# One decoder block kernel on one core: the front runs into the inversion without a barrier, two kinds of small transfers change queue, and value rows change places with a norm

## The reference

```python
p = rmsnorm(x, norm_mix) @ w_in            # 1024 -> 2048 (retention) + 1824 (RWKV)
q = rope(q, positions); k = rope(k, positions) * HEAD_DIM ** -0.5   # retention
# RWKV-7, one step per token
sa = einsum('bhvk,bhk->bhv', state, a_t)
state = state * w_t + sa[..., None] * b_t + v_t[..., None] * k_t
# second block: differential attention normalizes q and k over 32 features
q = rmsnorm_2(q, g_q); k = rmsnorm_2(k, g_k)
s = q @ k.T * scale + _t5_bias(table, dist)
```

## Time and profile before

| | us |
|---|---|
| median of three timed runs | 1727.69 (1725.25 to 1728.7) |
| the profiled execution, its own time | 1724.9 |
| its span in the trace | 1723.0 |
| busy in the span: PE, DVE, ACT, POOL | 1633.6, 902.3, 660.9, 75.7 |
| shares of the chain that ended last: PE, DVE, ACT, DMA | 82%, 6%, 6%, 1% |

### The profile page before, as it was taken

The page is one execution under the profiler, slowest core; times in us unless marked ns, Lnnn a source line. Parts: engine busy times, 40 slices in busy tenths (PEclk is TensorE's granted clock), DMA queues, the critical chain, the costliest instruction groups (busy, mean ns, idle before and its releaser), DMA issues.

```text
span 1723.0 us, 25989 instructions
## 1 busy us (share of the span) xinstructions
PE 1633.6 (95%) x11207; PEld 1311.3 (76%) x11207; DVE 902.3 (52%) x1404; ACT 660.9 (38%) x990; POOL 75.7 (4%) x105
## 2 busy tenths in 40 slices
PE   7899988999998999999999999996889999999998
PEld 5766768977796778888888777775557788888887
DVE  6444567515444355555454645434864765555544
ACT  3215931234434254333241435444775422222220
POOL 1300100000000000000000200002300000000000
PEclk9999998999999999999999999996989999999999
DMA  6612141003242344536363341420002233333322
GB/s 210 172 49 73 52 150 33 4 5 112 82 147 74 107 143 149 193 119 208 113 220 122 122 130 56 99 73 25 1 13 72 65 102 95 96 103 93 98 86 86
DMA packets 150692, 170.28 MB, mean 99 GB/s; under 512 B 14297, under 2 KB 111203, under 8 KB 150195
## 3 DMA queue, kind: packets, MB, share of 16 engines
q1 hardware_dynamic: 141080, 151.58, 27.7%
q10 hardware_dynamic: 9498, 17.06, 3.5%
HBM read 164.12 MB, written 6.33 MB: 99 GB/s over the span
## 4 chain that ended last, share of the span: by engine, by line
PE 82%; DVE 6%; ACT 6%; issue 2%; ACTq 1%; DMA 1%; POOL 1%; DVEq 0%; POOLq 0%; SPq 0%
PE ps L389 64%; PE ps L1250 4%; PE ps L1410 2%; PE ps L2371 1%; DVE weights_low L412 1%; PE ps L2383 1%; PE ps L2559 1%; ACT weights_high L409 1%; PE ps L2394 1%; PE ps L1636 1%; ACT sb_hT L2474 1%; DMA sb_arena<-sb_arena 1%; PE ps L894 1%; PE ps L906 1%; ACT sb_arena L671 1%
## 5 line engine op out<-in xcount | busy, mean ns | idle before, releaser
L389 PE MATMUL ps<-left_high,weights_high 128*128 128x512 f32 (+1 forms) x1016 | 403.4, 397 | 7.9 <-DVE left_low L693 3.3
L412 DVE TENSOR_TENSOR weights_low<-sb_weights_raw,weights_high 128x2048 fp32r<-128x2048 f32 (+1 forms) x118 | 265.2, 2248 | 260.7 <-ACT weights_high L409 260.6
L389 PE MATMUL ps<-left_high,weights_low 128*128 128x512 f32 (+1 forms) x1016 | 395.8, 390 | 0.0
L389 PE MATMUL ps<-left_low,weights_high 128*128 128x512 f32 (+1 forms) x1016 | 395.7, 389 | 0.0
L409 ACT CAST weights_high<-sb_weights_raw 128x2048 fp32r<-128x2048 f32 (+1 forms) x118 | 221.4, 1876 | 348.9 <-PE ps L389 294.0
L389 PEld LDWEIGHTS ps<-left_high,weights_high 128*128 128x128 f32 (+1 forms) x1016 | 190.0, 187 | 63.4 <-issue 13.4
L389 PEld LDWEIGHTS ps<-left_high,weights_low 128*128 128x128 f32 (+1 forms) x1016 | 190.1, 187 | 41.0
L389 PEld LDWEIGHTS ps<-left_low,weights_high 128*128 128x128 f32 (+1 forms) x1016 | 190.2, 187 | 40.3 <-issue 1.7
L389 PE MATMUL ps<-weights_high,hidden_high 128*128 128x512 f32 x432 | 169.0, 391 | 0.0
L389 PE MATMUL ps<-weights_high,hidden_low 128*128 128x512 f32 x432 | 168.2, 389 | 0.0
L389 PE MATMUL ps<-weights_low,hidden_high 128*128 128x512 f32 x432 | 168.1, 389 | 0.0
(11 more groups left out here) (394 smaller groups left out, 2134.3 us busy)
## 6 DMA issues: line engine op xcount, KB each, us to landing
sb_weights_raw<-in_w_in SPq DMA_DIRECT2D x25, 1024.0 KB, 5.3
sb_yT<-in_ada_w SPq DMA_DIRECT2D x24, 1024.0 KB, 5.2
sb_weights_raw<-in_ffn_w_up SPq DMA_DIRECT2D x44, 512.0 KB, 4.7
sb_weights_raw<-in_mlp_w_up SPq DMA_DIRECT2D x16, 1024.0 KB, 6.3
sb_weights_raw<-in_mlp_w_down SPq DMA_DIRECT2D x16, 1024.0 KB, 7.6
sb_weights_raw<-in_ffn_w_down SPq DMA_DIRECT2D x10, 1024.0 KB, 5.0
sb_weights_raw<-in_xattn_w_kv SPq DMA_DIRECT2D x8, 1024.0 KB, 5.1
sb_weights_raw<-in_w_out SPq DMA_DIRECT2D x6, 1024.0 KB, 5.0
```

What stands on the lines that cost most here:

```text
L389: last = nc.tensor.matmul(o, lhsT, rhs, start=b["first"] and i == 0, stop=b["last"] and i == len(pairs) - 1)
L412: nc.vector.tensor_tensor(l[:, 0:n], raw[:, 0:n], h[:, 0:n].bitcast(F32), ALU.subtract).then_inc(w_low, 1)
```

## The change

The edits are five.

- The barrier between the front and the inversion is gone on the three engines. In its place stand waits: TensorE waits for ScalarE's copies of the last two chunks, and before each u for a count `removal_ready`, which VectorE raises once per BT tile and once per bonus tile (u 0 and 1 need one and two, u 2 and 3 all eight). The bonus sums lie in banks 2, 3, 6 and 7 instead of 2 to 5, since u 0 and 1 write banks 0, 4, 1 and 5. ScalarE waits for the last product of `w_in` before the two gate DMAs.
- The eight DMAs of the skewed table are issued by SyncE, ahead of the third chunk of `w_q`.
- The four DMAs of the keys' exchange are issued by SyncE, behind the load of chunk 7 of `w_in`. Those of the queries stay with ScalarE.
- ScalarE takes its 18 steps there in one piece.
- VectorE takes five dense steps behind each of the two norms, where it took two.

```diff
         def bonus_pe(pe, f):
...
-            nc.tensor.matmul(ps[:, 2 + f, :], sum64, BON_IN[:, f % 2, :], start=True, stop=True).then_inc(bonus_sum, 1)
+            nc.tensor.matmul(ps[:, BONUS_BANK[f], :], sum64, BON_IN[:, f % 2, :], start=True,
+                             stop=True).then_inc(bonus_sum, 1)
...
-            swap_act(a, 0)
-            fill(dense, 8)
-            swap_act(a, 1)
-            fill(dense, 10)
+            exchange_halves(a, a.eng, 0)
+            fill(dense, 18)
...
         def invert_pe(pe):
+            for n in (-2, -1):
+                kept_by_act(pe, w_in, n)
             for u in range(NPAIR):
+
+                pe.wait_ge(removal_ready, (u + 1, u + 1, 8, 8)[u])
                 chunk_products(u, of_cols(BT), of_cols(AT), u).then_inc(inv_gram, 1)
...
         def invert_act(a):
+            a.wait_ge(acc_done, w_in[-1]["blocks"][-1]["acc"])
             a.eng.dma_start(GUP0, A["rwkv_g_up"][0, 0:P]).then_inc(front_loaded, 16)
             a.eng.dma_start(GUP1[0:32], A["rwkv_g_up"][0, P:P + 32]).then_inc(front_loaded, 16)
-            skew_bias_act(a)
...
-                fill(dense, 2)
+                fill(dense, 5)
...
-            stream_weights(sp, STREAM[1:])
+            stream_weights(sp, STREAM[1:8])
+            exchange_halves(sp, sp, 1)
+            stream_weights(sp, STREAM[8:w_qkv[2]["index"]])
+            skew_bias_sp(sp)
+            stream_weights(sp, STREAM[w_qkv[2]["index"]:])
...
             front1_pe(pe)
-            pe.stage_end()
             invert_pe(pe)
```

More of the change, by code:

```diff
@@ L542, in store_bias_act, with skew_bias_sp @@
             a.eng.dma_start(bias_dram, VECS[0:8]).then_inc(bias_stored, 16)
-        def skew_bias_act(a):
+        def skew_bias_sp(sp):
+            sp.wait_ge(bias_stored, 16)
             for h in range(8):
@@ L548, in skew_bias_act @@
                 rows = bass.AP(tensor=bias_dram.tensor, offset=h * VEC, ap=[[0, P], [1, VEC]])
-                a.eng.dma_start(skewed, rows).then_inc(bias_stored, 16)
+                sp.dma_start(skewed, rows).then_inc(bias_stored, 16)
         def load_params_sp(sp):
@@ L839, in rot_tile @@
             return (QT, KTt)[n // 4][:, n % 4, :]
-        def swap_act(a, q_or_k):
+        def exchange_halves(side, queue, q_or_k):
             src = (QT, KTt)[q_or_k]
-            kept_by_act(a, w_in, 2 * q_or_k + 1)
+            kept_by_act(side, w_in, 2 * q_or_k + 1)
             if q_or_k:
-                a.wait_ge(rotated, 4)
+                side.wait_ge(rotated, 4)
             for to in range(0, P, 32):
                 frm = to + 32 if to % 64 == 0 else to - 32
-                a.eng.dma_start(EXCHANGED[to:to + 32], src[frm:frm + 32]).then_inc(swapped, 16)
+                queue.dma_start(EXCHANGED[to:to + 32], src[frm:frm + 32]).then_inc(swapped, 16)
         def rotate_dve(v, n):
@@ L977, in build_program @@
         (lora_in, lora_w, lora_a, sig_w, sig_a, kk_squared, kk_scaled, kk_sum, kk_floor,
[L978 removed]
+         removal_ready, kk_rstd, key_scale, key_scaled, cum_ready, before_ready, decay_w, decay_before, decay_inv, bonus_in,
          bonus_sum) = (sem("rwkv_" + n) for n in (
              "lora_in", "lora_w", "lora_a", "sig_w", "sig_a", "kk_squared",
[L981 removed]
+             "kk_scaled", "kk_sum", "kk_floor", "removal_ready", "kk_rstd", "key_scale", "key_scaled", "cum_ready", "before_ready",
              "decay_w", "decay_before", "decay_inverse", "bonus_in", "bonus_sum"))
@@ L1080, in removal_dve @@
             v.wait_ge(decay_inv, f + 1)
-            nc.vector.tensor_tensor(BT[:, f, :], AA[:, f, :], WI[:, f, :], ALU.mult)
+            nc.vector.tensor_tensor(BT[:, f, :], AA[:, f, :], WI[:, f, :], ALU.mult).then_inc(removal_ready, 1)
         def receptance_dve(v, f):
@@ L1095, in receptance_dve @@
             nc.vector.tensor_tensor(KTW[:, f, :], KTW[:, f, :], WI[:, f, :], ALU.mult)
+        BONUS_BANK = (2, 3, 6, 7)
         def bonus_pe(pe, f):
@@ L1105, in bonus_dve @@
             v.wait_ge(acc_done, w_in[-1]["blocks"][-1]["acc"])
-            nc.vector.tensor_tensor(BON[:, f, :], ps[:, 2 + f, :], VT[:, f, :], ALU.mult)
+            nc.vector.tensor_tensor(BON[:, f, :], ps[:, BONUS_BANK[f], :], VT[:, f, :], ALU.mult).then_inc(removal_ready, 1)
         def front1_pe(pe):
@@ L3061, in _ @@
             front1_act(a)
-            a.stage_end()
             invert_act(a)
```

3 lines of the change are left out of this document (removed).

## The result

| | before | changed |
|---|---|---|
| median, us | 1727.49 | 1715.34 |
| lowest to highest, us | 1725.25 to 1728.70 | 1711.92 to 1717.84 |
| profiled execution, us | 1724.9 | 1717.84 |
| its span, us | 1723.0 | 1716.0 |

The account below looks back on a forecast made before the run. The prediction took TensorE, with 82% of the chain, to bound the kernel, with gains only where it waits. Its terms -9.0 - 6.9 + 1.4 = -14.5 us gave 1713.2 us against the 1727.69 median, 8-in-10 range 1707 to 1719.5.

Parts of the forecast that it names:

- the forecast's own case: Whole kernel: the predicted 1713.2 us, own range 1709 to 1717.5, chance 0.65.
- Two of the signs that the forecast named for being wrong: Retention starting before 90 or after 95; attention stage longer by more than 2 us; a third was a `w_q` wait.
- The norm, -9.0: Second norm: copies placed before it shorten TensorE's idle time from 11.7 to 3.1 us; 9.0 us less.
- The inversion, -6.9: Inversion's start: VectorE starts at 246.5 instead of 253.40, 6.2 us from the table DMAs, the rest from the barrier.
- the forecast's upper bound: Inversion's start: at most 7.8 us gained, if the gate DMAs too were off the path.
- The tables on SyncE, 0: SyncE's queue near `w_q`: eight table copies delay no weights; third chunk lands about 437, cast at 451.22; cost nothing.
- The front, +1.4: Keys' exchange behind chunk 7: lands at 82.5, retention starts at 92.3, lower clock costs 1.6 us; front 1.4 us later.
- the forecast's strict sum: Keys' exchange queued wholly behind chunk 7 (78.6, then 4.7 us) lands at 83.3; the sum is 0.8 us worse.
- The exchange comes late: Rival, front: exchange lands at 88, retention starts at 97.8; sum -9.0 us, 1718.7 us; chance 0.14.
- The inversion does not start earlier: Rival, inversion: only the barrier's 0.06 us go; sum -7.6 us, 1720.1 us; chance 0.05.
- the tables block the weights: Rival, SyncE's queue: table copies make the third `w_q` chunk late; slower, 1736 us at 80 GB/s; chance 0.04.
- Both early gaps close: Rival, front and norm: exchange lands near 79.6, c8 at full clock; sum -20.7 us, 1707 us; chance 0.12.

Follow-up runs that it names:

- again: The changed kernel measured a second time, with no edit: 1713.55 us.
- e2: Changed kernel with the keys' exchange still on SyncE, but ahead of chunk 7's load instead of behind it: 1704.12 us.
- e5: Changed kernel with the barrier between front and inversion put back on three engines, tables still on SyncE: 1718.25 us.
- e9: Kernel before with only the inversion part of the change, no barrier and the tables on SyncE: 1721.26 us.
- e1: Changed kernel with the keys' exchange issued by ScalarE again, as in the kernel before: 1709.47 us.
- e6: Kernel before with one edit, five value-row copies instead of two between the norms: 1720.51 us.
- e10: Kernel before with only the front part, the keys' exchange on SyncE behind chunk 7's load: 1731.54 us.
- e11: e8 with one more edit, chunk 5's weights split on VectorE ahead of the rotations: 1697.03 us.
- e7: Changed kernel with six value-row copies instead of five before the second norm's four multiplications: 1708.64 us.
- e8: Changed kernel with the edits of e2 and e7 together: 1702.03 us.

## Why the prediction was right, and where not

The time, 1715.34 against 1713.2, is in the range of the forecast's own case, and in part by luck. Of its terms one was too small and one was nearly right for partly wrong reasons. By the marks the three parts give -9.0 - 7.9 + 5.8 = -11.1 us (-11.5 with the 5.4 of "again"), against -14.5 forecast and -12.2 in the medians. The front's term was 4.4 us too good and the inversion's 1.0 too poor; the first miss alone would have made 1717.6 of 1713.2, at the edge of the range, and the rest was made up by the second and by scatter. Two of the signs that the forecast named for being wrong came about: retention started at 95.53, after 95, and the attention stage was 4.3 us longer in the profiled execution, more than 2. The first shows a real miss, in the front; the second belongs mostly to the execution ("again").

**The norm, -9.0.** Measured 9.0 (16.78 to 7.79), with c8 at 1177.33 - 1172.66 = 4.67 us, near the 4.93 that the forecast took from the kernel before. It named both ends rightly. TensorE's clock over c8, in the changed kernel and in e2, shows the two:

```profile
1172.66:1177.33 4.67, 4.63 (x24) 4.43 (x24) 0.28 (x2) 0.00 (x0) 0.00 (x0) 0.63 0.00 0
1163.30:1166.47 3.17, 3.13 (x24) 2.92 (x24) 0.28 (x2) 0.00 (x0) 0.00 (x0) 1.00 0.00 0
```

In e2 and e5 the granted clock stayed at 1.00 behind the same 3.02 us of idleness, and the norm took 6.30 us. That it fell in the changed kernel, as assumed, was not certain.

**The inversion, -6.9.** Measured 7.9; the forecast's upper bound was 7.8, for the case that the gate loads too are off the path, and they are. The split is another than it said. With the tables on ScalarE the barrier's removal takes 10.31 to 7.59; with them on SyncE, 5.30 to 2.40: 2.7 and 2.9 us. The tables are worth 10.31 to 5.30 and 7.59 to 2.40: 5.0 and 5.2. The forecast gave 6.2 and 0.7. It counted the barrier as the time between its last arrival and the next instruction. It is more than that: TensorE could not form the first products while VectorE multiplied bonus tiles, and that was hidden in the kernel before only by the tables. The gate loads, at 0.87 us, fell off the path since without the barrier they are issued beside ScalarE's last front work. The Trainium skill, page "DMA: Bandwidth & Descriptors", section "Issuing engines are not separate DMA queues", calls the issue time that another engine takes over usually small beside the transfer itself. The trace agrees as far as that goes (5.16 us of issues for some 17 us of transfers), but those 5 us were the whole price here, as the issues stood ahead of a copy that all waited for and nobody waited for the transfers.

**The tables on SyncE, 0.** Right, with the third chunk landed at 433.1 (forecast 437, which is 432.8 in this trace's time) and a cast that waits for nothing.

**The front, +1.4.** This step failed by size. To VectorE's first row sum it is 5.8 us in the first trace. Counted from the first weights, the seven traces with this front take 66.9 (e5) to 69.6 us (changed) to there, against 64.1 in the kernel before and 63.9 to 66.2 in e9, e1 and e6 with its order, so the cost is 2.9 to 5.6 by the execution. In the time, e10 gives 4.4 alone and e1 5.9 or 4.1 the other way. The steps, in the first trace: TensorE's stall at 72 us went, as was said. Chunk 7 was issued at 74.4 instead of 73.3. It took 7.1 us instead of the 5.3 that the forecast took from a load with nothing behind it, and landed at 81.5 instead of 78.6. The exchange landed 4.3 us behind it, at 85.8; the forecast's strict sum had 4.7, and then took 0.8 off for an overlap. An overlap there was, but it only made chunk 7 later. The DMA engines are busy throughout (share 0.90 and 0.93 in the two windows) and move 5 x 253 + 4 x 206 KB = 2.09 MB from 75 to 84 us, all the bytes of chunk 7 and of the exchange. The Trainium skill, same page, section "Queues, rings and completion order", has descriptors of one queue consumed in ring order. The traces agree on who lands first, here and in e2; the forecast stated the rule and then chose a landing 0.8 us ahead of its own sum by it. So retention started 3.2 us later than forecast (95.53 against 92.3). The lower clock then cost 2.8 us (5.8 - 3.0) instead of 1.6, since TensorE worked at it for some 6 us and not 3.4 as in the kernel before (76.8 to 80.2). 3.2 and 1.2 are the whole difference.

The forecast also had TensorE through with its products at 86.8; it was 89.33. It waits 1.85 us for chunk 5's split near 67 us (0.9 in the kernel before), and at 68 to 70 us its granted clock is 0.50, so that it reaches its new stall later. That cost nothing here, since retention waited for the exchange, and e11 takes the wait away.

**The attention stage** had no term, but the forecast named 2 us for a lower clock at its start. In its first 5 us the granted clock is 0.62 in both traces of the changed kernel and was 0.73 before, and yet in thirteen of fourteen traces the stage takes 116.0 to 117.3 us, before as after, whatever stands ahead of it.

**The rivals.** "The exchange comes late" had a landing of 88 and 1718.7; the truth, 85.81, lies between it and the forecast. "The inversion does not start earlier" and "the tables block the weights" fell with the rows above. "Both early gaps close" did not come about, though e2 and e7 close them by edits.

**What stays open.** The parts alone sum to -6.6 - 5.8 + 4.4 = -8.0 us, the whole change to -12.2 and -13.8. Each of these has an interval of about 2.6 us to either side, so the gap may be scatter; that is not shown. The marks don't show any part working less alone: 7.79 for the norm in e6 and 2.40 for the inversion in e9. What differs is elsewhere: in e6 the front, the same code as before, was 2.1 us later (99.28), and the stretch to the norm took 903.2 us instead of 899.6, with a granted clock of 0.97 in one of its windows,

```profile
1100.00:1160.00 60.00, 58.63 (x383) 44.56 (x383) 22.45 (x30) 33.80 (x33) 0.00 (x0) 0.97 0.25 75
```

and e5 and e8 have 901.6 and 900.9 there. Why such dips come in some executions was not tried.

## What to carry to other kernels

Before a transfer is moved to another queue, ask what will be ahead of it there, and put an urgent small one ahead of a bulk load that nobody waits for yet: against the changed kernel the place in the queue was worth 9 to 11 us, and 6.6 between e7 and e8, while e2 and e1, with another engine as the issuer, are 5.4 apart. A barrier's cost is not the gap between its last arrival and the next instruction (0.06 us here, against the 2.7 to 2.9 measured), but what its waiters could have done since their own last input; it shows only once the work that covers it is gone. Where one engine serves a queue of copies and a late step, count the copies that are ready before that step's input is, and place exactly these ahead of it: five were worth 9 us, six another 5.

## What was not expected of the hardware

Four transfers of 256 KB from SBUF to SBUF, issued in 2.57 to 3.11 us, landed 6.9 us after the first issue with nothing ahead of them (e2) and 10.9 us after it behind a 1 MB load, and that load took 7.1 us with them behind it, 5.2 alone. The clock is not told by the length of TensorE's idleness alone: 1.08 us (e2, at retention) left it at its full level; behind 1.9 us near 67 us it was 1.00 in e2 and 0.50 in the changed kernel; behind 3.02 us, the same in all traces with five copies, one block took 4.67 us in some executions and in two, e2 and e5, 1.5 us less; behind 6.20 us it stayed at 0.50 for some 6 us of work. Eight copies of 512 KB from HBM to HBM on the weights' queue took some 17 us (an estimate from 412 to 429) and delayed no weights. The same kernel's executions differ by 6 to 7 us (1711.92 to 1717.84 and 1712.36 to 1719.74), more than some of the edits studied here are worth.
